# Chunk inputs of a state-space stage as four 32-row tiles on the plain input, instead of block-expanded copies of it

## The chip, the cores and the metric

The kernel runs on one core of a Trainium2 chip. The metric is the device time of one execution in microseconds (us). Engines are named as in the profile: PE is TensorE (PEld its weight loads), DVE is VectorE, ACT is ScalarE, POOL is GpSimd, SP is SyncE.

## The reference

One inference step of a two-layer decoder trunk. Layer 0 has a diagonal state-space mixer (S5), layer 1 latent attention, and each has a gated feed-forward before and behind its mixer. There are 512 prompt tokens and 8 sample tokens, 520 in all, of width 1024. Everything is float32. The change is in the mixer of layer 0:

```python
# 64 groups of 16 channels; each group has 64 complex states
ug = uf.reshape(b_, n, N_GROUPS, GROUP_CH)
x_re = jnp.einsum('bngc,gpc->bngp', ug, bb_re)
x_im = jnp.einsum('bngc,gpc->bngp', ug, bb_im)
...
_, _, s_re, s_im = lax.associative_scan(combine, (l_re, l_im, x_re, x_im), axis=1)
y = einsum(s_re, c_re) - einsum(s_im, c_im)
```

The state is carried over positions by `s = lam * s + x`. The kernel cuts the 512 positions into 64 chunks of L = 8, and first works out what each chunk adds to the state at its end: the sum over i of `lam^(7-i) * B * u[8c+i]`. These sums are the chunk inputs.

## The kernel before, in words

`u` holds the normalised input as 8 tiles t of 128 channels (8 groups, that is QP = 4 pairs of groups, of 32 channels each). Its 512 prompt columns are ordered (i, c), position in the chunk first, so that `u[:, t, i*64:(i+1)*64]` is position i of all 64 chunks; columns 512 to 519 are the sample tokens.

For each tile t four engines work in a chain:

- PE `powers_in(t)`: two matmuls of 64 rows by 512 columns (L1784), one of 64 by 128 (L1785) and two of 128 by 64 (L1787) bring the powers of lam, a factor and B into PSUM banks 4 to 6. It waits until tile t-1's were read.
- ACT copies them out (`lpz` L775, `fz` L776), DVE multiplies them (L1255 to L1267) into `bp`, and ACT spreads `bp` into the stationary operand `wb` (L782, two instructions). `wb` has two buffers by t % 2, `bp` one. DVE starts tile t when ACT has spread tile t-1.
- PE forms the chunk inputs (L1814, L1816). A stationary tile of `wb` has 128 rows (channels) and 128 columns (2 groups x 64 states). It is the same 128 columns for each of the four pairs, so a pair must see only its own 32 channels. Before, that is done by a block-expanded copy of the input, `ue`: for each of the 8 positions i, 128 rows x (4 pairs x 64 chunks), in which pair q's 64 columns are zero but for its own 32 rows. One matmul then serves four pairs. `use` is the same for the sample tokens.
- ACT copies the chunk inputs out of PSUM (`chunk_inputs`, L767 and L768). Its program has them one tile late: copies of tile t, `wb` of t, chunk inputs of t-1, copies of t+1.

DVE makes `ue` and `use` with eight copies a tile (`blocks(t)`, L1236 and L1237): those of tiles 0 and 1 ahead of the loop, those of t+1 behind the products of t. POOL clears both once (L2291), at 283 us, while PE works on the first feed-forward.

PE's order in the stage is `powers_in(0)`, and then for each t `powers_in(t+1)`, chunk inputs of t. Once four tiles are copied out, POOL scans pairs 0 to 15 (`chunk_scan`, L445 to L449); once all are, DVE scans pairs 16 to 31. PE goes on when DVE's scan is done.

A float32 matmul of the program stands in the trace as two records of PE and two of PEld. So the 8 matmuls of L1814 are 16 records.

Of the kernel before, what the change touches and what calls it, by code (L numbers as in the profile page):

```python
# [19 lines left out]
F32 = mybir.dt.float32  # L20
# [4 lines left out]
ACT = mybir.ActivationFunctionType  # L25
AX = mybir.AxisListType

P = 128
D = 1024
KD = D // P  # L30
SEQ = 512
NB = 8
TOK = SEQ + NB
# [3 lines left out]
NF = FF // P  # L37
# [6 lines left out]
L = 8  # L44
NCH = SEQ // L
NBK = 8
SCAN_T = 4
QP = 4
# [51 lines left out]
NSS = len(S_STEPS)  # L100
AFTER_CH = 2 * NPG * (R + DR) - (NQT + 2 * RT) * TOK
XQ = 48

INV2PI = 1.0 / (2.0 * math.pi)
MAGIC = 12582912.0
# [92 lines left out]
def yoco_step(nc, inp, out):  # L198
# [4 lines left out]
    with ctx:  # L203
        def take(scope, *tensors):
            return [scope.enter_context(nc.sbuf_tensor(*t)) for t in tensors]

        def sem(name):
            return ctx.enter_context(nc.semaphore(name))


        with ExitStack() as end:
            yo, yso = take(end, ("yo", [P, 4, D], F32), ("yso", [NB, D], F32))
        with ExitStack() as s:

            ue, use = take(s, ("ue", [P, 2, L, QP, NCH], F32), ("use", [P, 2, QP, NB], F32))
        xh, xl = take(ctx, ("xh", [P, KD, TOK], F32R), ("xl", [P, KD, TOK], F32R))
        x, sq, ta, tb, cst, gain, cT, kpT, ones, epsc, sd, rstd, rstc, rbc = take(
            ctx, ("x", [P, KD, TOK], F32), ("sq", [P, 2, TOK], F32), ("ta", [P, 2, TOK], F32),
# [15 lines left out]
        with ExitStack() as s:  # L234
            u, xs, bz, cz, s0, sn, lpz, fz = take(
                s, ("u", [P, KD, TOK], F32), ("xs", [P, 2, NPAIR, NCH + 1], F32), ("bz", [P, KD, 2, NS], F32),
                ("cz", [P, 2, KD, NS], F32), ("s0", [P, 2, NPAIR, NB], F32), ("sn", [P, 2, NPAIR, NB], F32),
                ("lpz", [P, 2, 2, L * NS], F32), ("fz", [P, 2, 2 * NS], F32))
            with ExitStack() as a:
                bnat, be, bp, wb, pr = take(  # L240
                    a, ("bnat", [P, 2, NPAIR, GC], F32), ("be", [P, 2, KD, P], F32), ("bp", [P, L, 2, NS], F32),
                    ("wb", [P, 2, L, 2, P], F32), ("pr", [P, 2, L * NS], F32))
# [32 lines left out]
        ps = ctx.enter_context(nc.psum_tensor("ps", [P, 8, 512], F32))  # L275


        xsm = tb[:, 0, 0:2 * NPAIR * NB].rearrange("p (r n b) -> p r n b", r=2, n=NPAIR)
# [3 lines left out]
        def prm(j, n=1):  # L282
# [19 lines left out]
        w_hi, w_lo, w_used = sem("w_hi"), sem("w_lo"), sem("w_used")  # L302
# [4 lines left out]
        std_rdy, rstd_rdy, rb_rdy = sem("std_rdy"), sem("rstd_rdy"), sem("rb_rdy")  # L307
        xn_rdy, xh_rdy, xl_rdy = sem("xn_rdy"), sem("xh_rdy"), sem("xl_rdy")
        f_sig, f_g, f_u, f_t, f_h, f_hi, f_lo, g_sig = (sem(n) for n in ("f_sig", "f_g", "f_u", "f_t", "f_h", "f_hi", "f_lo", "g_sig"))
        m_zero, d_o2, t_in, s_cz, s_ue, s_uz = sem("mla_zero"), sem("dec_o_head"), sem("trig_in"), sem("s5_ct_zero"), sem("s5_u_blocks"), sem("s5_u_zero")  # L310
        s_cpi, s_lam = sem("s5_cp_im"), sem("s5_lam_done")
        dch, ach, gch = sem("dch"), sem("ach"), sem("gch")
        pa, pd, pe_p = sem("par_act"), sem("par_dve"), sem("par_pe")
        s_in, s_tr, s_u, s_z, s_be, s_mu, s_e, s_ev, s_bb, s_bp, s_wb, s_x, s_xe = (sem("s5_" + n) for n in (
            "in", "tr", "u", "zero", "be", "mu", "lam", "lam_sb", "bb", "bp", "wb", "x", "x_sb"))
# [286 lines left out]
        def _(act):  # L602
            own = Chain(act, ach)
            run = nc.scalar.activation
# [158 lines left out]
            def chunk_inputs(t):  # L763

                act.wait_ge(s_x, t + 1)
                x_ps = ps[:, 2 * (t % 2):2 * (t % 2) + 2, :]
                run(xs[:, :, QP * t:QP * t + QP, 1:NCH + 1], x_ps[:, :, 0:QP * NCH].rearrange("p r (q c) -> p r q c", q=QP), ACT.Copy)  # L767
                run(xsm[:, :, QP * t:QP * t + QP, :], x_ps[:, :, QP * NCH:QP * (NCH + NB)].rearrange("p r (q c) -> p r q c", q=QP), ACT.Copy).then_inc(s_xe, 1)  # L768

            for t in range(KD):  # L770

# [9 lines left out]
                for h in range(2):  # L781
                    last = run(wb[:, t % 2, :, :, h * NS:h * NS + NS], bp[:, :, :, :], ACT.Copy, scale=cst[:, C_PAR + h:C_PAR + h + 1])  # L782
# [125 lines left out]
            for h in range(2):  # L908
                for r in range(RT):
                    last = run(qlat[:, r, :, h:NH:2], ps[:, 2 + h, r * NH // 2 * NB:(r + 1) * NH // 2 * NB].rearrange("p (i b) -> p b i", b=NB), ACT.Copy)  # L910
# [117 lines left out]
        def _(dve):  # L1028
            own = Chain(dve, dch)
            V = nc.vector  # L1030
            tt, stt, ts, copy = V.tensor_tensor, V.scalar_tensor_tensor, V.tensor_scalar, V.tensor_copy
# [191 lines left out]
            for w in range(2):  # L1223
                for h in range(2):
                    for c, r, sign in ((0, 0, 1.0), (1, 1, 1.0), (2, 1, -1.0), (3, 0, 1.0)):
                        first = (2 * w + r) * NG + h
                        last = ts(lst[NS * h:NS * h + NS, w, c, :], ps[0:NS, 3, first:first + NG - 1:2], sign, None, ALU.mult)
            last.then_inc(pe_p, 1)

            def blocks(t):  # L1230

                if t >= 2:
                    dve.wait_ge(s_x, t - 1)
                for q in range(QP):
                    rows = slice(32 * q, 32 * q + 32)
                    copy(ue[rows, t % 2, :, q, :], u[rows, t, 0:SEQ].rearrange("p (i c) -> p i c", i=L))  # L1236
                    last = copy(use[rows, t % 2, q, :], u[rows, t, SEQ:TOK])  # L1237
                last.then_inc(s_ue, 1)

            dve.wait_ge(s_u, KD)  # L1240
            dve.wait_ge(s_uz, 1)
            blocks(0)
            blocks(1)
            for t in range(KD):

                dve.wait_ge(s_z, t + 1)
                if t >= 1:
                    dve.wait_ge(s_wb, t)
                b_ps = ps[:, 6, P:2 * P].rearrange("p (r s) -> p r s", r=2)

                def f_(r):
                    return fz[:, t % 2, r * NS:r * NS + NS].unsqueeze(1).to_broadcast([P, 2, NS])

                q0, q1 = (pr[:, r, 0:2 * NS].rearrange("p (r s) -> p r s", r=2) for r in range(2))
                tt(q0, f_(0), b_ps, ALU.mult)  # L1255
                last = tt(q1, f_(1), b_ps, ALU.mult)
                last.then_inc(s_bb, 1)
                dve.wait_ge(s_bb, t + 1)
                tt(bz[:, t, 0, :], q0[:, 0, :], q1[:, 1, :], ALU.subtract)
                own(tt(bz[:, t, 1, :], q0[:, 1, :], q1[:, 0, :], ALU.add))  # L1260
                copy(bp[:, 0, :, :], bz[:, t, :, :])
                p0, p1 = (pr[:, r, 0:(L - 1) * NS].rearrange("p (j s) -> p j s", s=NS) for r in range(2))
                for r in range(2):
                    lam = [lpz[:, t % 2, i, 0:(L - 1) * NS].rearrange("p (j s) -> p j s", s=NS) for i in range(2)]
                    tt(p0, lam[0], bz[:, t, r:r + 1, :].to_broadcast([P, L - 1, NS]), ALU.mult)
                    own(tt(p1, lam[1], bz[:, t, 1 - r:2 - r, :].to_broadcast([P, L - 1, NS]), ALU.mult))
                    last = tt(bp[:, 1:L, r, :], p0, p1, ALU.add if r else ALU.subtract)  # L1267
                    if r == 0:
                        own(last)
                last.then_inc(s_bp, 1)  # L1270
                if 1 <= t < KD - 1:
                    blocks(t + 1)


            dve.wait_ge(s_mu, 1)
            dve.wait_ge(s_xe, KD)
# [143 lines left out]
            for k in range(4):  # L1420
                for h in range(4):
                    last = copy(qpe[DR * k:DR * k + DR, :, k, Q_POS[h]:NH:4], qq[DR * h:DR * h + DR, NH // 2:NQT, SEQ:TOK].rearrange("p g b -> p b g"))
# [133 lines left out]
            for r in range(RT):  # L1556
                own(tt(new, nwt[:, :, 0:NH], cT[:, r, SEQ:TOK].unsqueeze(2).to_broadcast([P, NB, NH]), ALU.mult))
                last = tt(olat[:, r, :, :], new, ps[:, 5 + r, 0:NB * HP].rearrange("p (b h) -> p b h", b=NB)[:, :, 0:NH], ALU.add)
# [4 lines left out]
            for h in range(2):  # L1563
                last = copy(of[DV * h:DV * h + DV, :, :],
                            ps[DV * h:DV * h + DV, 0, 0:NH * NB].rearrange("p (n b h) -> p n b h", n=NH // 2, b=NB)[:, :, :, h])
# [22 lines left out]
        def _(pe):  # L1588
            mm = nc.tensor.matmul
# [49 lines left out]
            for k in range(KD):  # L1639
                got = turn(ps[:, 5, k * NB:k * NB + NB], xsin[:, k * P:k * P + P], NB)  # L1640
# [157 lines left out]
            for t in range(KD):  # L1798
                if t + 1 < KD:
                    powers_in(t + 1)  # L1800
                pe.wait_ge(s_wb, t + 1)
                pe.wait_ge(s_ue, t + 1)
                if t == 1:
                    pe.wait_ge(pe_p, 2)
                if t >= 2:
                    pe.wait_ge(s_xe, t - 1)
                elif t == 0:
                    pe.wait_ge(s_ev, 1)


                for r in range(2):
                    x_ps = ps[:, 2 * (t % 2) + r, :]
                    for i in range(L):
                        mm(x_ps[:, 0:QP * NCH], wb[:, t % 2, L - 1 - i, r, :], ue[:, t % 2, i, :, :].rearrange("p q c -> p (q c)"),  # L1814
                           start=i == 0, stop=i == L - 1, skip_group_check=True)
                    got = mm(x_ps[:, QP * NCH:QP * (NCH + NB)], wb[:, t % 2, 0, r, :], use[:, t % 2, :, :].rearrange("p q c -> p (q c)"),  # L1816
                             start=True, stop=True, skip_group_check=True)
                got.then_inc(s_x, 1)


# [419 lines left out]
        def _(pool):  # L2240
            own = Chain(pool, gch)
            G = nc.gpsimd
# [44 lines left out]
            G.memset(prm(12), 0.0).then_inc(s_lam, 1)  # L2287


            pool.wait_ge(w_used, 2 * NF)  # L2290
            G.memset(ue[:, :, :, :, :], 0.0)  # L2291
            G.memset(use[:, :, :, :], 0.0).then_inc(s_uz, 1)
            pool.wait_ge(s_uz, 1)


            pool.wait_ge(x_upd, UPD["ffn00"] + KD)
            own(G.memset(be[:, :, :, :], 0.0))
            pool.wait_ge(s_in, 128)
# [96 lines left out]
```

## Time and profile before

| | |
|---|---|
| time, median of 3 runs (lowest, highest) | 2413.15 us (2410.35, 2415.62) |
| the profiled execution: its time, its span | 2413.23 us, 2411.6 us |
| PE, DVE, ACT, POOL busy | 2239.7, 1098.4, 774.4, 220.1 us |
| chain that ended last | PE 85%, DVE 8%, ACT 3% |
| L1814 PE, 256 records | 63.2 us |
| the stage of the change | from 430 to 531 us of the span |

The busy rows say how long each engine had something in flight. The chain is the row of instructions that ended last, followed back from the end. The granted clock (PEclk) is the share of TensorE's full 2.4 GHz: 1.00, or 0.50, which is 1.2 GHz.

### The profile page before, as it was taken

The page shows a single profiled execution, that of the slowest core. Times are in us where ns is not written, and L with a number is a line of the kernel's source. Part 1 is how long each engine was busy: PE and PEld are TensorE (multiplying, and loading weights), DVE is VectorE, ACT ScalarE, POOL GpSimd, SP SyncE. Part 2 cuts the span into 40 slices and gives each one's busy share as a digit, 9 for nine tenths or more (in the row PEclk, how much of TensorE's full clock was granted, in tenths as well). Part 3 has the DMA queues.
Part 4 walks back from the last instruction along what each step waited for, and adds up shares of the span by engine and source line. Part 5 has one row for each costly group of instructions (what it writes and reads, how often), then busy time and mean ns, then how long its engine had stood idle before and what let it go on. Part 6 is the DMA issues. An engine that isn't in the chain of part 4 may idle for free.

```text
span 2411.6 us, 45473 instructions
## 1 busy us (share of the span) xinstructions
PE 2239.7 (93%) x18959; PEld 2079.7 (86%) x18959; DVE 1098.4 (46%) x1583; ACT 774.4 (32%) x1079; POOL 220.1 (9%) x319
## 2 busy tenths in 40 slices
PE   7999999872999999999999999998898789999998
PEld 7999998651669999999999999997565579999998
DVE  5445422776553454442255444223575324445432
ACT  4343311220332444332242222224354314443311
POOL 4000000183320000000000000000004500000000
PEclk9999999795999999999999999999899979999999
DMA  4332333000003233333223333221125702332332
GB/s 118 88 95 87 104 89 76 16 0 5 2 10 97 79 88 95 90 100 94 74 87 89 96 87 107 84 72 66 46 55 141 203 27 78 88 96 87 104 86 84
DMA packets 355907, 192.30 MB, mean 80 GB/s; under 512 B 33004, under 2 KB 350442, under 8 KB 355794
## 3 DMA queue, kind: packets, MB, share of 16 engines
q1 hardware_dynamic: 348736, 180.19, 26.2%
q0 software_dynamic: 5488, 9.03, 1.4%
q10 hardware_dynamic: 1570, 1.48, 0.2%
q8 instruction: 82, 1.34, 0.2%
q14 instruction: 31, 0.25, 0.0%
HBM read 184.23 MB, written 3.02 MB: 78 GB/s over the span
## 4 chain that ended last, share of the span: by engine, by line
PE 85%; DVE 8%; ACT 3%; issue 2%; SPq 1%; DMA 1%; POOL 0%; ACTq 0%; DVEq 0%
PE ps L1602 70%; PE ps L1615 3%; PE ps L1814 2%; PE ps L1880 1%; PE ps L1944 1%; PE ps L2069 1%; DVE pr L445 1%; PE ps L2100 1%; PE ps L1831 1%; SPq L419 1%; PE ps L1621 1%; SPq L417 1%; PE ps L2047 1%; DVE wl L1039 1%; DMA cb<-cache_ckv 1%
## 5 line engine op out<-in xcount | busy, mean ns | idle before, releaser
L1602 PE MATMUL ps<-xh,wh 128*128 128x260 f32 x3296 | 869.0, 285 | 16.6 <-DVE wl L1054 8.9
L1602 PE MATMUL ps<-xl,wh 128*128 128x260 f32 x3296 | 862.3, 283 | 0.0
L1602 PE MATMUL ps<-xh,wl 128*128 128x260 f32 x3296 | 666.1, 284 | 0.0
L1602 PEld LDWEIGHTS ps<-xh,wh 128*128 128x128 f32 x3296 | 625.7, 190 | 23.7 <-issue 14.8
L1602 PEld LDWEIGHTS ps<-xl,wh 128*128 128x128 f32 x3296 | 623.8, 189 | 0.0
L1602 PEld LDWEIGHTS ps<-xh,wl 128*128 128x128 f32 x3296 | 510.9, 190 | 0.0
L640 ACT ACTIVATE wh<-raw 128x1024 fp32r<-128x1024 f32 (+1 forms) x176 | 194.3, 1104 | 609.0 <-PE ps L1602 609.0
L1602 PE MATMUL ps<-hh,wh 128*128 128x260 f32 x1408 | 370.3, 284 | 0.0
L1602 PE MATMUL ps<-hl,wh 128*128 128x260 f32 x1408 | 367.5, 282 | 0.0
L1602 PE MATMUL ps<-hh,wl 128*128 128x260 f32 x1408 | 283.3, 282 | 0.0
L1602 PEld LDWEIGHTS ps<-hh,wh 128*128 128x128 f32 x1408 | 264.9, 188 | 4.4 <-issue 4.2
L1602 PEld LDWEIGHTS ps<-hl,wh 128*128 128x128 f32 x1408 | 265.6, 189 | 0.0
L1054 DVE TENSOR_TENSOR wl<-raw,wh 128x1024 fp32r<-128x1024 f32 (+1 forms) x176 | 225.1, 1279 | 77.5 <-ACT wh L640 77.5
L1039 DVE TENSOR_TENSOR wl<-raw,wh 128x1024 fp32r<-128x1024 f32 (+1 forms) x98 | 136.0, 1387 | 231.7 <-ACT wh L622 231.7
L622 ACT ACTIVATE wh<-raw 128x1024 fp32r<-128x1024 f32 (+1 forms) x98 | 116.6, 1189 | 380.4 <-PE ps L1602 379.3
L1602 PEld LDWEIGHTS ps<-hh,wl 128*128 128x128 f32 x1408 | 217.1, 188 | 0.0
L1132 DVE TENSOR_TENSOR sq<-ps,rbc 128x520 f32<-128x520 f32 x88 | 61.6, 700 | 286.5 <-PE ps L1602 286.5
L1127 DVE TENSOR_TENSOR ta<-ps,rbc 128x520 f32<-128x520 f32 x88 | 61.6, 700 | 174.6 <-PE ps L1602 173.9
L1166 DVE SCALAR_TENSOR_TENSOR x<-ps,x 128x520 f32<-128x520 f32 (+1 forms) x32 | 22.4, 700 | 175.4 <-PE ps L1602 175.4
L700 ACT ACTIVATE hh<-ta 128x520 f32 (+1 forms) x88 | 56.4, 640 | 96.4 <-DVE ta L1136 96.4
L1814 PE MATMUL ps<-ue,wb 128*128 128x256 f32 x256 | 63.2, 404 | 7.7 <-ACT wb L782 7.7
L1814 PEld LDWEIGHTS ps<-ue,wb 128*128 128x128 f32 x256 | 50.4, 202 | 15.3 <-ACT wb L782 8.3
(362 smaller groups left out, 2219.0 us busy)
## 6 DMA issues: line engine op xcount, KB each, us to landing
raw<-ffn_w_gate SPq DMA_DIRECT2D x88, 512.0 KB, 3.9
raw<-ffn_w_up SPq DMA_DIRECT2D x88, 512.0 KB, 3.9
raw<-ffn_w_down SPq DMA_DIRECT2D x64, 704.0 KB, 4.6
cb<-cache_ckv SPq DMA_DIRECT2D x72, 128.0 KB, 2.9
cb<-cache_ckv POOLq DMA_DIRECT2D x56, 128.0 KB, 3.1
raw<-s_w_glu_v SPq DMA_DIRECT2D x8, 512.0 KB, 3.8
raw<-s_w_glu_g SPq DMA_DIRECT2D x8, 512.0 KB, 3.8
raw<-mla_w_o SPq DMA_DIRECT2D x8, 512.0 KB, 4.3
```

The costliest lines, as they stand in the source:

```text
L417: eng.dma_start(cb[j][:, g, :], inp["cache_ckv"][bass.ds(numbers[b][g], 1)].rearrange("a p r -> p (a r)")).then_inc(arrived[j], 16)
L419: eng.dma_start(kb[j][:, g, :], inp["cache_kpe"][bass.ds(numbers[b][g], 1)].rearrange("a p r -> p (a r)")).then_inc(arrived[j], 16)
L622: run(wh[par_][:, 0:size], raw[par_][:, 0:size], ACT.Copy).then_inc(w_hi, 1)
L640: run(wh[par_][:, 0:size], raw[par_][:, 0:size], ACT.Copy).then_inc(w_hi, 1)
L700: run(hh[:, bass.ds(f, 1), :].rearrange("p a t -> p (a t)"), ta[:, j, :], ACT.Copy).then_inc(f_hi, 1)
L1039: tt(wl[par_][:, 0:size], raw[par_][:, 0:size], wh[par_][:, 0:size], ALU.subtract).then_inc(w_lo, 1)
L1054: tt(wl[par_][:, 0:size], raw[par_][:, 0:size], wh[par_][:, 0:size], ALU.subtract).then_inc(w_lo, 1)
L1127: tt(halves(ta[:, j, :]), banks(0), halves(rbc[:, :]), ALU.mult).then_inc(f_g, 1)
L1132: tt(halves(sq[:, j, :]), banks(2), halves(rbc[:, :]), ALU.mult).then_inc(f_u, 1)
L1602: got = mm(ps[0:width, bank + half, 0:HALF], w[par_][:, k * width:k * width + width], src[:, k0 + k, half * HALF:half * HALF + HALF], star ...
L1615: return nc.tensor.transpose(dst, src, ident[0:rows, 0:rows])
L1814: mm(x_ps[:, 0:QP * NCH], wb[:, t % 2, L - 1 - i, r, :], ue[:, t % 2, i, :, :].rearrange("p q c -> p (q c)"), start=i == 0, stop=i == L - ...
```

## The change

`ue` and `use` are gone, with POOL's clearing and DVE's copies. PE takes the stationary and the moving operand of one pair from the same 32 rows of `wb` and of the plain `u`. So each matmul of L1814 becomes four, of 32 rows by 64 columns, and each of L1816 four of 32 rows by 8. They stand one after the other in the program, on four different row groups of the array, and write four different PSUM banks (pair q goes to bank q). All of a tile lies in columns 0 to 143 of banks 0 to 3, real part and imaginary part behind one another. Before, tiles alternated between banks 0, 1 and 2, 3. So a tile's chunk inputs now wait until ACT has copied out those of the tile just ahead, not of the one ahead of that.

```diff
+XW = NCH + NB
-            ue, use = take(s, ("ue", [P, 2, L, QP, NCH], F32), ("use", [P, 2, QP, NB], F32))
@@ ACT
-                x_ps = ps[:, 2 * (t % 2):2 * (t % 2) + 2, :]
-                run(xs[:, :, QP * t:QP * t + QP, 1:NCH + 1], x_ps[:, :, 0:QP * NCH].rearrange("p r (q c) -> p r q c", q=QP), ACT.Copy)
-                run(xsm[:, :, QP * t:QP * t + QP, :], x_ps[:, :, QP * NCH:QP * (NCH + NB)].rearrange("p r (q c) -> p r q c", q=QP), ACT.Copy).then_inc(s_xe, 1)
+                x_ps = ps[:, 0:QP, 0:2 * XW].rearrange("p q (r w) -> p r q w", r=2)
+                run(xs[:, :, QP * t:QP * t + QP, 1:NCH + 1], x_ps[:, :, :, 0:NCH], ACT.Copy)
+                run(xsm[:, :, QP * t:QP * t + QP, :], x_ps[:, :, :, NCH:XW], ACT.Copy).then_inc(s_xe, 1)
@@ DVE
-            def blocks(t):
-                if t >= 2:
-                    dve.wait_ge(s_x, t - 1)
-                for q in range(QP):
-                    rows = slice(32 * q, 32 * q + 32)
-                    copy(ue[rows, t % 2, :, q, :], u[rows, t, 0:SEQ].rearrange("p (i c) -> p i c", i=L))
-                    last = copy(use[rows, t % 2, q, :], u[rows, t, SEQ:TOK])
-                last.then_inc(s_ue, 1)
-            dve.wait_ge(s_u, KD)
-            dve.wait_ge(s_uz, 1)
-            blocks(0)
-            blocks(1)
...
-                if 1 <= t < KD - 1:
-                    blocks(t + 1)
@@ PE
-                pe.wait_ge(s_ue, t + 1)
...
-                if t >= 2:
-                    pe.wait_ge(s_xe, t - 1)
-                elif t == 0:
+                if t >= 1:
+                    pe.wait_ge(s_xe, t)
+                else:
                     pe.wait_ge(s_ev, 1)
                 for r in range(2):
-                    x_ps = ps[:, 2 * (t % 2) + r, :]
+                    c = r * XW
                     for i in range(L):
-                        mm(x_ps[:, 0:QP * NCH], wb[:, t % 2, L - 1 - i, r, :], ue[:, t % 2, i, :, :].rearrange("p q c -> p (q c)"),
-                           start=i == 0, stop=i == L - 1, skip_group_check=True)
-                    got = mm(x_ps[:, QP * NCH:QP * (NCH + NB)], wb[:, t % 2, 0, r, :], use[:, t % 2, :, :].rearrange("p q c -> p (q c)"),
-                             start=True, stop=True, skip_group_check=True)
+                        for q in range(QP):
+                            rows = slice(32 * q, 32 * q + 32)
+                            mm(ps[:, q, c:c + NCH], wb[rows, t % 2, L - 1 - i, r, :], u[rows, t, i * NCH:(i + 1) * NCH],
+                               start=i == 0, stop=i == L - 1, skip_group_check=True)
+                    for q in range(QP):
+                        rows = slice(32 * q, 32 * q + 32)
+                        got = mm(ps[:, q, c + NCH:c + XW], wb[rows, t % 2, 0, r, :], u[rows, t, SEQ:TOK],
+                                 start=True, stop=True, skip_group_check=True)
                 got.then_inc(s_x, 1)
@@ POOL
-            pool.wait_ge(w_used, 2 * NF)
-            G.memset(ue[:, :, :, :, :], 0.0)
-            G.memset(use[:, :, :, :], 0.0).then_inc(s_uz, 1)
-            pool.wait_ge(s_uz, 1)
```

On PE, at `powers_in(1)` and the chunk inputs of tile 0, there stands before (the shape is that of the output, `x8` is eight in a row):

```order
L1784 MATMUL ps<-lpw,cst 128x512 x2
L1785 MATMUL ps<-fcm,cst 128x128
L1787 MATMUL ps<-cst,be 128x64 x2
L1814 MATMUL ps<-ue,wb 128x256 x8
L1816 MATMUL ps<-use,wb 128x32
L1814 MATMUL ps<-ue,wb 128x256 x8
L1816 MATMUL ps<-use,wb 128x32
```

and in the changed kernel, whose lines are numbered 19 lower here:

```order
L1765 MATMUL ps<-lpw,cst 128x512 x2
L1766 MATMUL ps<-fcm,cst 128x128
L1768 MATMUL ps<-cst,be 128x64 x2
L1796 MATMUL ps<-u,wb 128x64 x32
L1800 MATMUL ps<-u,wb 128x8 x4
L1796 MATMUL ps<-u,wb 128x64 x32
L1800 MATMUL ps<-u,wb 128x8 x4
```

Nothing has changed places: 18 matmuls a tile have become 72. On DVE, between the products of tile 1 and those of tile 2, there stands before:

```order
L1267 TENSOR_TENSOR bp<-pr 128x7x64
L1236 COPY ue<-u 32x8x64
L1237 COPY use<-u 32x8
L1236 COPY ue<-u 32x8x64
L1237 COPY use<-u 32x8
L1236 COPY ue<-u 32x8x64
L1237 COPY use<-u 32x8
L1236 COPY ue<-u 32x8x64
L1237 COPY use<-u 32x8
L1255 TENSOR_TENSOR pr<-fz,ps 128x128
```

and in the changed kernel, where the same products are L1249 to L1251 and L1239 to L1240:

```order
L1249 TENSOR_TENSOR pr<-lpz,bz 128x448
L1250 TENSOR_TENSOR pr<-lpz,bz 128x448
L1251 TENSOR_TENSOR bp<-pr 128x7x64
L1239 TENSOR_TENSOR pr<-fz,ps 128x128
L1240 TENSOR_TENSOR pr<-fz,ps 128x128
```

Here the eight copies are gone, and tile 2's products follow tile 1's.

## Rows read from the trace of the kernel before

**Rows 1.** Stretches: PE, PEld, DVE, ACT, POOL busy (records), PEclk, DMA share, GB/s.
```profile
430.00:445.40 15.40, 10.44 (x20) 5.52 (x20) 12.83 (x42) 3.34 (x5) 8.20 (x16) 0.50 0.01 1
445.40:450.60 5.20, 5.11 (x12) 4.14 (x13) 3.92 (x10) 1.11 (x3) 0.00 (x0) 0.50 0.00 2
458.00:468.00 10.00, 10.00 (x48) 8.04 (x48) 6.55 (x19) 3.97 (x6) 0.00 (x0) 1.00 0.00 0
```

**Rows 2.** PE's timeline: start, us from first start to last end, line, records, idle before.
```profile
437.87 3.75 PE L1784 MATMUL ps<-lpw,cst 64*128 64x512 f32 x4 [2.61 <-DVE pr L1256]
...
441.98 1.11 PE L1787 MATMUL ps<-cst,be 128*128 128x64 f32 x4
445.49 6.24 PE L1814 MATMUL ps<-ue,wb 128*128 128x256 f32 x16 [2.40 <-ACT wb L782]
...
458.10 3.67 PE L1814 MATMUL ps<-ue,wb 128*128 128x256 f32 x16
...
465.52 1.98 PE L1784 MATMUL ps<-lpw,cst 64*128 64x512 f32 x4
...
468.14 3.67 PE L1814 MATMUL ps<-ue,wb 128*128 128x256 f32 x16
...
500.57 5.41 PE L1814 MATMUL ps<-ue,wb 128*128 128x256 f32 x16 [2.12 <-ACT wb L782]
```

**Rows 3.** Timeline of ACT and DVE, tile 0 and tile 2.
```profile
436.21 0.27 ACT L776 ACTIVATE fz<-ps 128x128 f32<-128x128 f32 x1
...
437.24 0.29 DVE L1255 TENSOR_TENSOR pr<-fz,ps 128x128 f32<-128x128 f32 x1
...
458.30 1.02 ACT L775 ACTIVATE lpz<-ps 128x1024 f32<-128x1024 f32 x1 [2.01 <-PE ps L1787]
...
459.52 0.29 DVE L1255 TENSOR_TENSOR pr<-fz,ps 128x128 f32<-128x128 f32 x1 [1.91 <-ACT fz L776]
...
464.28 2.19 ACT L782 ACTIVATE wb<-bp,cst 128x1024 f32<-128x1024 f32 x2 [4.79 <-DVE bp L1267]
...
466.37 0.57 ACT L767 ACTIVATE xs<-ps 128x512 f32<-128x512 f32 x1
```

**Rows 4.** Timeline of POOL, DVE and ACT, tiles 5 and 7.
```profile
487.31 1.70 POOL L445 TENSOR_TENSOR bnat<-ta,xs 128x256 f32<-128x256 f32 x2 [46.46 <-ACT tb L768]
...
489.66 0.29 DVE L1255 TENSOR_TENSOR pr<-fz,ps 128x128 f32<-128x128 f32 x1 [1.35 <-ACT fz L776]
...
498.33 2.19 ACT L782 ACTIVATE wb<-bp,cst 128x1024 f32<-128x1024 f32 x2 [8.70 <-DVE bp L1267]
...
515.90 0.29 DVE L1255 TENSOR_TENSOR pr<-fz,ps 128x128 f32<-128x128 f32 x1
...
521.03 2.19 ACT L782 ACTIVATE wb<-bp,cst 128x1024 f32<-128x1024 f32 x2 [5.61 <-DVE bp L1267]
```

**Rows 5.** Timeline: the scan of POOL and DVE, and PE behind it.
```profile
531.66 1.90 DVE L445 TENSOR_TENSOR pr<-ta,xs 128x256 f32<-128x256 f32 x2 [10.66 <-ACT tb L768]
...
556.25 1.52 POOL L2338 TENSOR_TENSOR sn<-sn,tb 128x512 f32<-128x512 f32 x1
...
564.69 1.02 DVE L445 TENSOR_TENSOR pr<-ta,xs 128x224 f32<-128x224 f32 x2
...
579.22 1.11 PE L1615 MATMUL ps<-cst,sn 128*128 128x128 f32 x4 [48.41 <-DVE xs L449]
```

**Rows 6.** L2005, pairs of 64-row tiles, elsewhere in the program.
```profile
L2005 PE MATMUL ps<-qq,ukT x64: 252/253/273, 1702.6 to 1706.1; 64*128 64x8 f32 x64
```

**Rows 7.** PE's timeline at L1873, four 32-column tiles.
```profile
606.43 2.00 PE L1873 MATMUL ps<-xs,ct 128*32 128x64 f32 x128
```

**Rows 8.** Stretches, columns as in 1: L2005; behind it; L2213 (128-row tiles, 32 columns).
```profile
1702.60:1706.30 3.70, 3.67 (x64) 3.65 (x64) 2.91 (x16) 0.00 (x0) 0.00 (x0) 1.00 0.47 109
1706.80:1712.00 5.20, 4.95 (x11) 2.29 (x12) 0.34 (x1) 1.92 (x6) 0.00 (x0) 0.50 0.56 157
...
1945.70:1952.40 6.70, 6.66 (x32) 6.66 (x32) 0.00 (x0) 0.00 (x0) 0.00 (x0) 0.50 0.00 1
```

More of the change, by code:

```diff
@@ L212, in yoco_step @@
             yo, yso = take(end, ("yo", [P, 4, D], F32), ("yso", [NB, D], F32))
-        with ExitStack() as s:
-            ue, use = take(s, ("ue", [P, 2, L, QP, NCH], F32), ("use", [P, 2, QP, NB], F32))
         xh, xl = take(ctx, ("xh", [P, KD, TOK], F32R), ("xl", [P, KD, TOK], F32R))
@@ L309, in yoco_step @@
         f_sig, f_g, f_u, f_t, f_h, f_hi, f_lo, g_sig = (sem(n) for n in ("f_sig", "f_g", "f_u", "f_t", "f_h", "f_hi", "f_lo", "g_sig"))
-        m_zero, d_o2, t_in, s_cz, s_ue, s_uz = sem("mla_zero"), sem("dec_o_head"), sem("trig_in"), sem("s5_ct_zero"), sem("s5_u_blocks"), sem("s5_u_zero")
+        m_zero, d_o2, t_in, s_cz = sem("mla_zero"), sem("dec_o_head"), sem("trig_in"), sem("s5_ct_zero")
         s_cpi, s_lam = sem("s5_cp_im"), sem("s5_lam_done")
```

## Prediction

> **What bounds the kernel now.** I read the stretches of the stage first. From 458 to 468 us, one tile, PE is busy all of 10.00 us at granted clock 1.00, while DVE has 6.55 and ACT 3.97 us of work [rows 1]. So up to tile 4 the stage goes at PE's pace. PE's timeline gives the pace: a tile's chunk inputs start at 458.10 and those of the next at 468.14, 10.04 us later [rows 2]. Of this, `powers_in` takes 2.62 (465.52 to 468.14) and the chunk inputs 7.42. The reader should also see the clock. It is 0.50 from 430 on and stays so until 450.6 [rows 1]. It has risen by the stretch at 458, and what PE ran before the rise was the first tile's chunk inputs, full 128-row matmuls of 256 columns.
>
> The second limit is the loop of ACT and DVE. For tile 2 [rows 3]: ACT's copy to DVE's first product 458.30 to 459.52, 1.22 us; products to `wb` at 464.28, 4.76; `wb` to the chunk-input copy at 466.37, 2.09; that copy about 0.8 (0.57 is its first part, the sample part behind it some 0.2). Together 8.9 us, 1.2 below PE's 10.04. From 487.31 POOL scans, and DVE's products slow down: 489.66 to 498.33, 8.67 us, for tile 5. For tile 7, when POOL is at its short instructions, they take 5.13 (515.90 to 521.03) [rows 4]. PE then waits. The stage ends into DVE's scan, which starts at 531.66 and releases PE at 579.22 [rows 5].
>
> **The change, part by part.** The profiled execution took 2413.23 us, the median of the runs is 2413.15, so the sum is made against 2413.2.
>
> 1. POOL's clearing at 283 us is gone. PE is in the first feed-forward there and waits for nothing of POOL's. Nothing.
>
> 2. DVE's copies. Those of tiles 0 and 1 lie ahead of the first product. Without them it waits for ACT's `fz`, done at 436.21 + 0.27 = 436.48, instead of starting at 437.24 [rows 3]: 0.7 us gained. The others lie beside PE's work up to tile 4. Their cover is PE's 10.04 us; should PE become short, the products could follow at once.
>
> 3. The chunk inputs on PE. A tile has 72 matmuls, so 144 records, in 36 sets of four on four row groups. The trace has no four 32-row tiles. Its nearest is L2005, 64-row tiles in alternating halves: 64 records in 3.67 us [rows 6, 8], 57 ns each. L2213, one 128-row tile after another, takes 6.66 us for 32 at clock 0.50 [rows 8], 208 ns each, so some 104 at full clock. Hence the two halves of L2005 work side by side, and each pair costs one load of 128 columns: 32 pairs at 115 ns. L1873, four 32-column tiles, has 128 records in 2.00 us, 16 ns each [rows 7], so four tiles side by side exist too. I take four at a time, a set at the price of one load, since a 32-row load has as many columns. That is 36 x 0.115 = 4.1 us at clock 1.00, and 36 x 0.208 = 7.5 at 0.50. Bounds: if the matmuls' 64 columns alone set the pace as in L1873, 144 x 16 ns = 2.3 us (4.6 at 0.50). If only two go side by side, 8.3 (15.0). If one at a time, 144 x 208 ns = 30 at 0.50.
>
> The Trainium skill (TensorE: Matmul & The Clock Gate, Back-to-back issue gap) has a rule against the change: with hardware decode off, the sequencer spends about 62 ns on each matmul. By it the tile would cost 144 x 62 ns = 8.9 us at any clock, not 4.1. The 16 ns of L1873 speak against that rule here.
>
> 4. The clock. This decides the sign. The new sets are paced by loads. Their matmuls stream 64 columns, 16 x 4 = 64 ns of every 115 by L1873's pace, so the array idles near half the time, though PE reads as busy. The trace has such streams. L2005 ran at 1.00, busy 3.67 of 3.70 us, nearly all of it loads, and the clock is 0.50 right behind it. L2213 ran 6.66 us without a gap and stayed at 0.50 [rows 8]. `powers_in`, whose long matmuls use 64 rows of the array, ran 3.75 us without a gap and stayed at 0.50 too [rows 1, 2]. The only thing that raised the clock in this stage was the 128-row stream from 445.49, and that is what is taken away. So I take 0.50 for the whole stage.
>
> 5. The sum at 0.50. `powers_in` takes 5.2 us (437.87 to 441.98 + 1.11) [rows 2], about 5.1 until the next can start. Chunk inputs 7.6 with their end. A tile: 12.7 us, against 10.04 before. Starts of the chunk inputs: tile 0 at 445.49 - 0.7 = 444.8; tile 1 at 457.5 (before 458.10, since tile 0 ran mostly at 0.50 then too); tile 4 at 457.5 + 3 x 12.7 = 495.6, before 458.10 + 3 x 10.04 = 488.2; tile 6 at 521.0, where its inputs have long been ready. Then the chain is DVE's: powers of tile 7 done about 521.1, copy 1.22, products 5.1, `wb` 2.1, chunk-input copy 0.8, so tile 7 starts at 530.4. It runs 7.9 to its result, the copy takes 0.8, and DVE's scan starts at 539.1 instead of 531.66: 7.5 us late. The new wait, for the copy of the tile just ahead, is hidden behind `powers_in`, except at tile 7, where the 0.8 stands in the sum.
>
> 6. What comes back. POOL's scan starts when tile 3 is copied, some 492.0 (`wb` of tile 4 from 489, done 491.2, then the copy) instead of 487.31: 4.7 late, while DVE's is 7.5 late. So they overlap 3 us less. Beside POOL DVE is slower: its pair of 256-column products takes 1.90 us, while 224 columns take 1.02 alone, which is 1.17 for 256, a factor of 1.63 [rows 5]. 3 us less overlap saves 3 x (1 - 1/1.63) = 1.1, and POOL, less disturbed in the slower stage, ends a little earlier still: 1.5 in all. Sum: 7.5 - 1.5 = 6 us slower, 2419.
>
> Where the clock rises behind the scan may shift: the same 16 records took 6.24 us with the rise in their course and 3.67 at full clock [rows 2], so one rise sooner or later is worth some 2.5 us either way. The forecast's own range is 2415 to 2425.
>
> **The rivals.**
>
> A. The clock rises all the same (0.15), since PE has hardly a gap. Then the loop of ACT and DVE paces the stage: 8.9 us a tile instead of 10.04, and tile 1 starts about 3.5 us earlier, as tile 0's chunk inputs shrink. By tile 4 that is 3.5 + 3 x 1.15 = 7 us, then 1 each for tiles 5 and 6, where DVE no longer copies, and 1 goes back to POOL: 8 us faster, 2405. It decides from a clock of 1.00 in about half of the stage on: each tile then gains where the forecast has it lose 2.7. Against it stand the three streams of step 4, and this: PE would now idle 8.9 - 2.6 - 4.1 = 2.2 us a tile, and after the idle 2.12 us at 500.57 sixteen records took 5.41 us instead of 3.67 [rows 2].
>
> The Trainium skill (same page, Part 1: The HAM clock gate) says that PE's activity releases the throttle and idling brings it back. If a busy PE is what it means, the stage would run at 2.4 GHz, and this rival would hold. L2213 was busy and was not released.
>
> B. Two tiles at a time, or one (0.14, of which 0.04 for one). L2005 shows two only. At 0.50 the chunk inputs take 15.0 us instead of 7.5, for eight tiles 60 more: 2413 + 6 + 60 = 2479. One at a time: 8 x 22.5 = 180 more, 2600. L1873's four column tiles speak against it.
>
> C. The loads hide and the 64 columns set the pace (0.05), 4.6 us at 0.50. A tile on PE is then 9.7, near the loop's 8.9; with the clock up the loop alone counts. Between no change and 8 us faster, 2407 as likeliest.
>
> **How the numbers follow.** The forecast has 0.66, A 0.15, B 0.14, C 0.05. What a measurement of this kernel tells from no change is about 0.2%, 4.8 us. Of the forecast's cases (6, give or take 2.5) a quarter fall within that: 0.17. So same is 0.17 and a little of C, 0.18; slower is 0.49 + 0.14 = 0.63; faster 0.19. The range leaves B out and reaches down to A: 2403 to 2425.
>
> **What the profile after would show.** PEclk 0.50 from 430 to the end of the scan (step 4). The changed L1814 in sets of four about 0.21 us apart, 7.5 us a tile (step 3). Chunk inputs 12.7 us apart, with PE busy throughout for tiles 1 to 6 (step 5). DVE's first product at 436.5 (step 2). POOL's scan starting about 492, DVE's about 539 (step 6). A clock of 1.00 there, or sets 0.4 us apart, would make the prediction wrong, each by the amount of its rival.

## The result, and the profile after

The changed kernel takes 2418.60 us (median of 17 runs, 2416.1 to 2428.3), the kernel before 2412.33 (17 runs in the same rounds, 2406.69 to 2415.82). The ratio is 1.0028, with a 95% interval of 1.0020 to 1.0036: a little slower, 6.3 us. The profiled execution of the changed kernel has a span of 2416.6 us, 5.0 more than before's 2411.6, and a mean granted clock of 0.941, where before had 0.959.

The first view is the page's row of the granted clock, one digit for each fortieth of the span (60.4 us):

```profile
PEclk9999999555999999999999999999899979999999
```

Before, the eighth, ninth and tenth digits were 7, 9 and 5. Now all three are 5. The stage ends in the ninth; the tenth belongs to the scan behind it and was 5 before too. TensorE now runs the whole stage at 1.2 GHz.

Stretches of the kernel after, columns as in [rows 1]:

```profile
430.00:445.40 15.40, 11.67 (x48) 6.71 (x48) 7.10 (x27) 4.45 (x6) 6.93 (x16) 0.50 0.01 1
445.40:450.60 5.20, 5.20 (x104) 5.20 (x101) 4.24 (x10) 0.75 (x1) 0.00 (x0) 0.50 0.02 3
458.00:468.00 10.00, 10.00 (x136) 8.28 (x133) 4.55 (x11) 3.09 (x6) 0.00 (x0) 0.50 0.01 2
450.00:535.00 85.00, 83.66 (x1037) 68.87 (x1036) 35.20 (x66) 26.52 (x40) 39.33 (x64) 0.50 0.01 2
```

PE is busy for 83.66 of 85 us and the clock stays at 0.50. In the stretch at 458 it had been 1.00 [rows 1]. In the 5.20 us from 445.40 on there are 104 matmul records, one every 50 ns.

PE's timeline of the kernel after, tiles 0 and 1, then the last two; columns as in [rows 2]:

```profile
444.04 3.69 PE L1796 MATMUL ps<-u,wb 32*128 32x64 f32 x64 [1.84 <-ACT wb L780]
...
451.83 3.78 PE L1765 MATMUL ps<-lpw,cst 64*128 64x512 f32 x4
...
457.01 3.69 PE L1796 MATMUL ps<-u,wb 32*128 32x64 f32 x64
...
521.94 3.69 PE L1796 MATMUL ps<-u,wb 32*128 32x64 f32 x64
...
531.14 3.69 PE L1796 MATMUL ps<-u,wb 32*128 32x64 f32 x64 [1.34 <-ACT tb L766]
...
584.90 1.12 PE L1596 MATMUL ps<-cst,sn 128*128 128x128 f32 x4 [45.89 <-DVE xs L447]
```

A tile's chunk inputs take 444.04 to 451.83, 7.79 us, and `powers_in` 5.18 more. The first halves of tiles 1 and 6 start 64.93 us apart, five tiles of 12.99 us, where before they were 10.04 apart [rows 2]. Only at tile 7 does PE wait. L1814 has become L1796, L1784 L1765, L1615 L1596; on DVE L1255 is L1239; on ACT and in the scans L782 and L445 are 2 lower.

The weight loads show how the sets of four go:

```profile
470.15 1.21 PEld L1796 LDWEIGHTS ps<-u,wb 32*128 32x128 f32 x20
...
L1796 PEld LDWEIGHTS ps<-u,wb x1024: 281/328/333, 444.0 to 538.2; 32*128 32x128 f32 x171
```

A load takes 328 ns, yet 20 of them take 1.21 us from the first start to the last end. Less the last one's 0.33 that is 0.88 us for four steps from set to set, 0.22 each. The four of a set start together, within some 0.02 us.

The scans, and DVE's first product:

```profile
436.35 0.29 DVE L1239 TENSOR_TENSOR pr<-fz,ps 128x128 f32<-128x128 f32 x1 [4.76 <-ACT fz L774]
...
491.98 1.46 POOL L443 TENSOR_TENSOR bnat<-ta,xs 128x256 f32<-128x256 f32 x2 [52.58 <-ACT tb L766]
...
539.88 1.98 DVE L443 TENSOR_TENSOR pr<-ta,xs 128x256 f32<-128x256 f32 x2 [11.70 <-ACT tb L766]
...
558.00 1.32 POOL L2316 TENSOR_TENSOR sn<-sn,tb 128x512 f32<-128x512 f32 x1
```

Against [rows 4, 5] POOL's scan starts 4.7 us later and ends 1.5 later. DVE's starts 8.2 later, and PE goes on 5.7 later (584.90 for 579.22). Two later lines of the kernel after show how far this delay lasts, L1989 (L2005 in the kernel before) and L2197 (L2213 there):

```profile
L1989 PE MATMUL ps<-qq,ukT x64: 252/253/273, 1708.6 to 1712.1; 64*128 64x8 f32 x64
...
L2197 PE MATMUL ps<-tb,ob x32: 401/401/422, 1950.1 to 1956.8; 128*128 128x32 f32 x32
```

At the first the kernel is 6.0 us late (before 1702.6 [rows 6]), at the second 4.4 (before 1945.7), at the end 5.0. What changes between 1700 us and the end lies in layer 1, whose program is the same in both. So 6.0 us is what the change costs in the two profiled executions, close to the 6.3 of the medians.

### The profile page after: what moved, and what is told of

It is laid out like the page before. It is cut to its first block, busy times and chain, and to the rows that moved or that the text cites. A ratio compares the mean times of both kernels' runs of the same rounds, so it can differ in the third digit from the quotient of the medians.

```text
span 2416.6 us, 47133 instructions
## 1 busy us (share of the span) xinstructions
PE 2254.0 (93%) x19823; PEld 2094.2 (87%) x19823; DVE 1072.9 (44%) x1519; ACT 774.7 (32%) x1079; POOL 211.7 (9%) x317
## 3 DMA queue, kind: packets, MB, share of 16 engines
q1 hardware_dynamic: 348736, 180.19, 26.1%
## 4 chain that ended last, share of the span: by engine, by line
PE 65%; DVE 3%; ACT 2%; SPq 1%; issue 1%; DMA 0%; DVEq 0%; ACTq 0%
PE ps L1583 54%; PE ps L1596 2%; PE ps L1928 1%; PE ps L2053 1%; PE ps L2084 1%; PE ps L1864 1%; SPq L415 1%; SPq L417 1%; PE ps L2031 1%; PE ps L1602 0%; DVE wl L1037 0%; ACT kk L921 0%; DVE mx L1423 0%; PE ps L2182 0%; PE ps L1609 0%
## 5 line engine op out<-in xcount | busy, mean ns | idle before, releaser
L1134 DVE TENSOR_TENSOR ta<-ta,sq 128x520 f32<-128x520 f32 x88 | 61.6, 700 | 3.0
L1796 PE MATMUL ps<-u,wb 32*128 32x64 f32 x1024 | 58.9, 419 | 3.2 <-ACT wb L780 1.8
```

Of the source, the lines that this page charges most:

```text
L1134: tt(ta[:, j, :], ta[:, j, :], sq[:, j, :], ALU.mult).then_inc(f_h, 1)
L1796: mm(ps[:, q, c:c + NCH], wb[rows, t % 2, L - 1 - i, r, :], u[rows, t, i * NCH:(i + 1) * NCH], start=i == 0, stop=i == L - 1, skip_group_c ...
```

## The experiments

The theory on trial: a set of four row tiles costs one load; this stream does not raise TensorE's clock, where the 128-row stream did; so the stage loses more by the clock than it gains by shorter chunk inputs. The rivals: the fineness itself costs (the number of instructions), the order of the tiles doesn't matter, or the copies on DVE mattered more than I said. x1 to x4 ran together and x5 to x8 together, each group with 23 runs of the kernel before beside it, 2413.49 and 2411.57 us in the median.

### x1_serial: the same matmuls with neighbours on the same rows

```diff
-                    for i in range(L):
-                        for q in range(QP):
-                            rows = slice(32 * q, 32 * q + 32)
-                            mm(ps[:, q, c:c + NCH], wb[rows, ...], u[rows, ...], ...)
                     for q in range(QP):
                         rows = slice(32 * q, 32 * q + 32)
+                        for i in range(L):
+                            mm(ps[:, q, c:c + NCH], wb[rows, ...], u[rows, ...], ...)
                         got = mm(ps[:, q, c + NCH:c + XW], wb[rows, ...], u[rows, t, SEQ:TOK], ...)
```

> The changed kernel with the order of its matmuls turned round: all eight positions of pair 0, then of pair 1, 2, 3, so that neighbours in the program use the same 32 rows of the array. Same matmuls, same banks. If the four-tile sets cost one load because they lie on four row groups (my reading), a tile now costs 144 x 0.208 = 30 us at clock 0.50 in place of 7.7, so eight tiles cost some 180 us more: about 2598. If what sets the pace is something else that the order doesn't touch (a fixed cost of each record, the 32-row form itself), the time stays at 2418.

Measured: 2554.63 us in one run, 136 above the changed kernel. PE's timeline, a stretch of it, and loads of one pair:

```profile
445.39 3.73 PE L1796 MATMUL ps<-u,wb 32*128 32x64 f32 x18 [1.81 <-ACT wb L780]
...
449.13 3.04 PE L1796 MATMUL ps<-u,wb 32*128 32x64 f32 x15
...
452.18 3.04 PE L1796 MATMUL ps<-u,wb 32*128 32x64 f32 x15
...
470.65 3.78 PE L1765 MATMUL ps<-lpw,cst 64*128 64x512 f32 x4
...
445.30:469.70 24.40, 24.31 (x140) 24.31 (x141) 4.55 (x11) 3.30 (x5) 0.00 (x0) 0.50 0.00 1
...
449.03 2.46 PEld L1796 LDWEIGHTS ps<-u,wb 32*128 32x128 f32 x11
```

The same 144 records take 25.3 us (445.39 to 470.65) instead of 7.79. PEld is busy throughout, and loads on the same rows follow one another: 11 in 2.46 us, less the last one's 0.33, is a step of 0.213. A whole set of four in the changed kernel takes such a step. So do 128-row loads in the kernel before, 31 steps in 6.6 us:

```profile
L2213 PEld LDWEIGHTS ps<-tb,ob x32: 288/333/333, 1945.7 to 1952.3; 128*128 128x128 f32 x32
```

Over eight tiles that is 8 x 17.5 = 140 us, and 136 were measured. So the four row groups working side by side are what makes a tile cost 7.8 us. Where my 2598 missed: a pair's 18 records take 3.05 us (449.13 to 452.18), not the 3.8 that 18 steps of 0.213 would need (3.7 with my 208 ns). At each change of rows some 0.8 us of the next pair's loads go beside the last ones of the pair ahead.

### x2_warm: the changed kernel with extra 128-row matmuls in PE's gaps

Results of the extra matmuls go to unused PSUM columns and nobody reads them. All else is computed as before.

```diff
+            def fill(n, bank=7, rows=P):
+                for _ in range(n):
+                    mm(ps[:, bank, P:3 * P], cst[0:rows, 0:P], x[0:rows, 0, 0:2 * P], start=True, stop=True, skip_group_check=True)
+            fill(7, 1)
             spread_rms("s5", SPLIT)
...
+            fill(3, 1)
             powers_in(0)
+            fill(4)
...
+                fill((10, 4, 4, 4, 4, 8, 8, 8)[t])
                 pe.wait_ge(s_wb, t + 1)
```

> The changed kernel with extra matmuls on PE whose results nobody reads: 128 rows by 256 columns, float32, in places where PE waits (7 and 3 ahead of the first powers, 4 behind them, then ahead of the chunk inputs of tiles 0 to 7: 10, 4, 4, 4, 4, 8, 8, 8). Theory: the change loses because the clock stays at 0.50 without the 128-row stream. Then these raise it to 1.00 before tile 0 and hold it; the sets come 0.11 us apart, the loop of ACT and DVE paces the stage at about 8.9 us a tile, and the time is about 2402. Rival: the row tiles are slow by themselves, or the clock can't be held over them; then the extra matmuls only lengthen PE's work and it ends at 2419 or above.

Measured: 2402.76 us (6 runs, 2399.41 to 2407.38), ratio to before 0.9963 (0.9949 to 0.9977). Stretches, then PE's timeline:

```profile
423.10:474.20 51.10, 47.30 (x703) 37.19 (x703) 32.76 (x84) 16.64 (x25) 10.93 (x21) 1.00 0.10 21
449.70:474.30 24.60, 24.53 (x480) 20.41 (x480) 13.27 (x33) 10.65 (x18) 0.00 (x0) 1.00 0.01 3
474.30:481.00 6.70, 6.70 (x16) 4.38 (x16) 1.88 (x5) 3.97 (x6) 3.12 (x5) 0.50 0.00 0
...
451.68 2.01 PE L1805 MATMUL ps<-u,wb 32*128 32x64 f32 x64
...
458.44 1.95 PE L1750 MATMUL ps<-x,cst 128*128 128x256 f32 x8
460.33 2.01 PE L1805 MATMUL ps<-u,wb 32*128 32x64 f32 x64
```

At clock 1.00 the 64 records take 2.01 us instead of 3.69, and a tile 8.65 us (451.68 to 460.33) although 1.95 of it are extras. That leaves 8.65 - 1.95 - 2.62 for `powers_in` [rows 2] = 4.1 us for a tile's chunk inputs. So at full clock the change gives a stage faster than before (10.04 a tile), and the sign hangs on the clock. The clock still fell at two places; the last of the three stretches is one. The expectation of x6_once says that PE had gaps there. At the first place it had none: in the 24.60 us ahead of the fall PE was busy for 24.53, with the row tiles, `powers_in` and four extra matmuls a tile.

### x5_fill64: the same extras on 64 rows

As x2_warm, with `rows=P // 2`.

> As the run that adds extra 128-row matmuls to the changed kernel (2402.8 us), in the same places and numbers, but each extra matmul uses 64 rows. PE is then as busy, only with half the array's rows. Theory: the powers, 64 rows too, never raised the clock, so these don't either; the clock stays at 0.50 through the stage, each extra matmul costs 0.85 us of PE's time, and with PE already the bound the whole is some 40 us longer than the changed kernel, about 2460. Rival: it is being busy without a gap that raises the clock; then as with 128 rows, about 2403.

Measured: 2458.23 us (4 runs), ratio 1.0182 (1.0158 to 1.0206). A tile's stretch, and the extras:

```profile
453.90:470.60 16.70, 16.70 (x163) 13.03 (x162) 2.25 (x8) 1.90 (x4) 0.00 (x0) 0.50 0.01 1
...
466.91 3.78 PE L1750 MATMUL ps<-x,cst 64*128 64x256 f32 x8
```

PE was busy for all of 16.70 us, and the clock was 0.50. As many matmuls with as many columns, on half of the rows, gave none of x2_warm's gain. So filled gaps by themselves don't help: with the 128-row extras the clock of this stage was at 1.00, with the 64-row extras in the same places at 0.50. A tile grew by the extras' own 3.8 us, and the whole by 40, as expected.

### x6_once: extras up to the first tile only

```diff
-                fill((10, 4, 4, 4, 4, 8, 8, 8)[t])
+                fill((10, 0, 0, 0, 0, 0, 0, 0)[t])
```

> The changed kernel with extra 128-row matmuls only up to tile 0 (7, 3, 4 and 10 of them), none after. Question: once raised, do the row tiles hold the clock? In the run with extras throughout, the clock fell to 0.50 behind tile 3 and in tile 6, where PE had gaps. Theory: without extras PE idles some 2.2 us a tile and the row tiles leave the array idle half of the rest, so the clock falls within the first tiles and nothing brings it back: 2410 to 2418. Rival: the row tiles hold it: about 2403, and the extras behind tile 0 were not needed.

Measured: 2412.73 us (10 runs), ratio 1.0006 (0.9995 to 1.0017). Stretches and PE's timeline:

```profile
436.70:453.50 16.80, 15.68 (x249) 12.58 (x252) 9.24 (x20) 7.12 (x10) 4.34 (x6) 1.00 0.00 1
453.70:462.90 9.20, 9.20 (x90) 6.79 (x86) 3.57 (x7) 2.78 (x4) 0.00 (x0) 0.50 0.00 1
475.90:532.00 56.10, 54.71 (x751) 47.17 (x750) 26.09 (x44) 15.89 (x24) 43.07 (x70) 0.50 0.01 1
...
451.68 2.01 PE L1805 MATMUL ps<-u,wb 32*128 32x64 f32 x64 [1.12 <-ACT tb L766]
...
475.91 3.69 PE L1805 MATMUL ps<-u,wb 32*128 32x64 f32 x64
```

The clock was 1.00 when the row tiles began, and fell in the course of the second. Then the pace is the changed kernel's again. The row tiles by themselves did not hold the clock here, nor did they bring it back (54.71 of 56.10 us busy at 0.50). PE had idled 1.12 us ahead of tile 1, so this run alone can't say whether they would have held it without any gap; but in x2_warm it fell once with no gap ahead. Each against the kernel before in its own rounds (1.0028, 1.0006 and 0.9963), the start alone was worth some 5 us of the 6.3 lost, and going on with the extras some 10 more.

### x3_before_warm: is the gain only that of a warm start?

The kernel before, with the same extras ahead of tile 0, and 4 each ahead of tiles 5, 6 and 7, where PE idles (`fill((10, 0, 0, 0, 0, 4, 4, 4)[t])`).

> The kernel before with the same extra matmuls up to tile 0 and 4 each ahead of tiles 5, 6, 7 (none at tiles 1 to 4, where PE has no gap). It shows what a warm start alone is worth, without the change. Expected: powers and tile 0 at clock 1.00, chunk inputs of tile 1 start about 6 us sooner, 2406. If it comes out as fast as the changed kernel with the extra matmuls (2402), the change has no gain of its own at full clock; I expect some 4 us between them.

Measured: 2413.80 us (12 runs), ratio 1.0000 (0.9988 to 1.0012). I had expected 2406. The timeline and stretches show why:

```profile
441.14 6.88 PE L1769 MATMUL ps<-x,cst 128*128 128x256 f32 x20
447.86 3.62 PE L1823 MATMUL ps<-ue,wb 128*128 128x256 f32 x16
...
439.10:445.80 6.70, 6.70 (x19) 5.06 (x18) 3.72 (x7) 2.85 (x3) 1.37 (x3) 0.50 0.00 0
446.00:530.00 84.00, 82.37 (x379) 67.13 (x378) 57.39 (x125) 26.74 (x42) 39.41 (x62) 1.00 0.00 1
```

The clock had fallen ahead of tile 0, where PE had waited for DVE, most of the extras ran at 0.50, and tile 0 started at 447.86 instead of 445.49. What it then saved at full clock (3.62 for 6.24 us [rows 2]) it had lost by starting late. From there on before had the clock at 1.00 too, but for a dip at 500.57 [rows 2], where ACT and DVE set the pace. So there was nothing left to win, whereas the row tiles had a whole stage at 0.50 to win back.

This profiled execution took 2405.01 us, 8.8 less than the median of the twelve (2404.28 to 2417.82). The stage has no part in that: PE went on behind the scan at 578.93, 0.3 us sooner than before. Two later lines show where the rest came from:

```profile
L2014 PE MATMUL ps<-qq,ukT x64: 252/253/273, 1701.7 to 1705.2; 64*128 64x8 f32 x64
...
L2222 PE MATMUL ps<-tb,ob x32: 401/401/422, 1937.6 to 1944.2; 128*128 128x32 f32 x32
```

Up to the first it was 0.9 us ahead of before (1702.6), at the second 8.1 (1945.7). Between them is attention of layer 1, the same program in both, so these 7 us are counted as scatter between executions. What extras are worth is better read at the end of the stage than from one execution's span.

### x4_nocopies: the kernel before without DVE's copies

In this kernel the chunk inputs of tiles 2 to 7 are made from the input of tiles 0 and 1; the eight copies of each later tile are left out.

```diff
-                if 1 <= t < KD - 1:
-                    blocks(t + 1)
...
-                pe.wait_ge(s_ue, t + 1)
+                pe.wait_ge(s_ue, min(t + 1, 2))
```

> The kernel before with DVE's block copies of tiles 2 to 7 left out, so the chunk inputs of those tiles are worked out from the wrong tile's data; everything else as before. It prices the part of the change that takes work off DVE. Theory: up to tile 4 the copies lie beside PE's work and cost nothing, at tiles 6 and 7 they hold DVE back by about 2 us, so 2410 to 2411, within 0.2% of before. Rival: the copies are what the stage waits for, then 4 us or more faster.

Measured: 2414.95 us (11 runs), ratio 1.0009 (1.0000 to 1.0019). Leaving DVE's copies out doesn't shorten the kernel. The timelines of DVE, PE and POOL:

```profile
502.29 0.29 DVE L1255 TENSOR_TENSOR pr<-fz,ps 128x128 f32<-128x128 f32 x1 [3.93 <-ACT fz L776]
...
513.24 6.66 PE L1812 MATMUL ps<-ue,wb 128*128 128x256 f32 x16 [2.35 <-ACT wb L782]
...
531.92 0.62 DVE L445 TENSOR_TENSOR pr<-ta,xs 128x256 f32<-128x256 f32 x1 [11.96 <-ACT tb L768]
...
554.38 1.39 POOL L2336 TENSOR_TENSOR sn<-sn,tb 128x512 f32<-128x512 f32 x1
```

DVE did begin tile 6's products at 502.29, 1.5 us sooner (503.80 before). But PE's wait for `wb` of tile 6 was 2.35 us, the clock was at 0.50 behind it, the sixteen records took 6.66 us, and DVE's scan began at 531.92, where before it was 531.66 [rows 5]. In this execution what DVE gained was lost by the clock, so the run doesn't price the copies apart from it. One thing did come of it: POOL's scan ended at 555.8 instead of 557.8 [rows 5]. It took 68.2 us (487.62 to 555.77), before 70.5 (487.31 to 557.77), and 70.4 and 70.8 in x3_before_warm and x8_before_scan, which have the copies. The copies had been slowing POOL.

### x7_warm_scan and x8_before_scan: both kernels with extras through DVE's scan too

x7 is x2_warm, x8 is x3_before_warm, both with

```diff
+            fill(104)
             pe.wait_ge(s_sn, 2)
...
             powers_out(0)
+            fill(14, 1)
             turn_out(0)
+            fill(5, 1)
```

> The changed kernel with the extras throughout the stage (2402.8 us), and more of the same kind where PE waits later: 104 during DVE's scan (44 us at full clock), 14 behind the first powers of the output part, 5 behind its first transposes. The clock should be 1.00 when the output part starts, where it is 0.50 for its first 25 us; two sets of powers, the transposes and the first taps each get 1 to 2 us shorter, together some 5: about 2397. If the extras outlast the scan or the clock falls in the gaps all the same, 2402 or above.

> The kernel before with the same extras as the run on the changed kernel with extras in the stage, the scan and the start of the output part. It shows whether the change itself, at the same clock, is worth something. The extras in the stage alone gave the kernel before nothing (2413.8 against 2413.5); those in the scan should give some 5 us: about 2408. Against 2397 for the changed kernel with them, 11 us between the two.

Measured: x7 2398.32 us (6 runs, 2393.67 to 2401.05), ratio 0.9939 (0.9923 to 0.9954), faster than both kernels; x8 2412.38 us (12 runs), ratio 0.9998 (0.9989 to 1.0007). x7, PE's timeline and a stretch:

```profile
518.68 43.11 PE L1750 MATMUL ps<-x,cst 128*128 128x256 f32 x199
...
568.14 3.78 PE L1825 MATMUL ps<-lpw,cst 64*128 64x512 f32 x4
...
584.99 1.98 PE L1825 MATMUL ps<-lpw,cst 64*128 64x512 f32 x4 [0.62 <-ACT bt L814]
586.90 3.70 PE L1852 MATMUL ps<-ct,bt 128*128 128x512 f32 x8
...
435.80:503.90 68.10, 65.24 (x1107) 53.17 (x1107) 40.00 (x77) 26.43 (x40) 29.45 (x34) 1.00 0.01 2
```

The kernel before, where those last two matmuls stand:

```profile
597.73 3.78 PE L1831 MATMUL ps<-lpw,cst 64*128 64x512 f32 x4 [2.78 <-ACT bt L816]
601.44 5.06 PE L1858 MATMUL ps<-ct,bt 128*128 128x512 f32 x8
```

In x7 the first powers behind the scan still took 3.78 us, since the clock had fallen in the 5 us of gap ahead of them; the second ones took 1.98 and the next matmuls 3.70, where before they took 3.78 and 5.06.

x8, the same two views as of x7:

```profile
447.30:580.20 132.90, 128.28 (x592) 107.21 (x590) 101.98 (x207) 27.24 (x42) 65.73 (x90) 1.00 0.00 1
...
586.13 8.49 PE L1769 MATMUL ps<-x,cst 128*128 128x256 f32 x28
```

With the clock at 1.00 in nearly all of the stage in both, the row tiles are 14 us faster than the block-expanded copies. Not all of that is the chunk inputs' own: tile 0 began at 449.56 in x8 and at 443.01 in x7. x8's own expectation, 2408, missed. As in x3, tile 0 began late, and behind the scan the clock fell all the same, so that the 28 extra records there cost 8.49 us.

## Why the prediction was right, step by step

The forecast of 2419 met 2418.6, and the mechanism was the one forecast: a set at the price of one load, at a clock that stays at 0.50. That the number met to half a microsecond is in part luck, since two terms were off and made up for each other: 7.5 - 1.5 was forecast, 8.2 - 2.5 came.

- **Steps 1 and 2, POOL's clearing and DVE's copies.** DVE's first product came at 436.35, 0.9 us sooner (0.7 predicted), and tile 0's chunk inputs at 444.04, 1.4 sooner than before (444.8 predicted). The rest is in tile 0's products, which took 5.4 us to `wb` (436.35 to 441.80) instead of 6.0 (437.24 to 443.25). That the copies beside PE's work cost nothing up to tile 4, x4_nocopies bears out: without them its tiles were 10.05 us apart there.
- **Step 3, a set of four at the price of one load.** Predicted 7.5 us a tile at clock 0.50 and 4.1 at 1.00; found 7.79 and 4.1. x1_serial shows that the row groups beside one another do it. The Trainium skill (TensorE: Matmul & The Clock Gate, Part 3: Packing small matmuls) says that a load overlaps matmuls in flight only where the row group is another. For loads on other row groups the traces agree, with 7.8 and 25.3 us for the same records. Whether a load on the same rows waits for the matmul ahead of it, no row here shows: in x1_serial it is one load after another, 0.213 us apart. Of rival B nothing is left.
- **The rule on the sequencer.** By the rule of the Trainium skill (same page, Back-to-back issue gap), 62 ns a matmul with hardware decode off, the tile was estimated at 8.9 us at any clock. The 7.79 us of the changed kernel and the 4.1 of x2_warm are below it. Which way decode was set, no run here shows.
- **Step 4, the clock.** 0.50 throughout, as said, and it decides the sign: x2_warm and x7_warm_scan are faster than before, and in x5_fill64 it stayed at 0.50 although PE was always busy. The Trainium skill (same page, Part 1: The HAM clock gate) has it that activity releases the throttle. With activity read as a busy PE, the trace disagrees: 83.66 of 85 us busy at 0.50. Rival A had its mechanism right and its condition wrong; its price, 2405, was near the 2402.8 of x2_warm, which has extras besides.
- **Step 5, the sum.** A tile takes 12.99 us, not 12.7, and DVE's scan came 8.2 us late, not 7.5. The sets are 0.216 us apart (7.79 / 36) where I had 0.208, which is 0.3 us a tile. The 0.208 was a misreading of [rows 8]: 6.66 us is the busy time of a stretch that ends before L2213's last record does. Its loads have a step of 0.213, as shown under x1_serial. From tile 1 to tile 6 that makes 5 x 0.29 = 1.5 us; tile 1 began 0.5 early (457.01 for 457.5), so tile 6 was 0.9 late against the forecast (521.94 for 521.0), and with it all that follows. The new wait for the tile just ahead cost what was said: at tile 7 `wb` was ready at 530.41 (528.22 + 2.19) and PE started at 531.14, behind ACT's copy. At full clock it counts at more tiles: in x7_warm_scan `wb` of tile 5 was ready at 488.90 and PE started at 489.64. An arrangement with two sets of PSUM columns wasn't tried.
- **Step 6, what comes back.** I had 1.5 us. It was 2.5: from DVE's start to PE's going on, 45.0 us (539.88 to 584.90), before 47.6. The term that I sized too small is the overlap with POOL. It is 19.4 us (539.9 to 559.3), before 26.1 (531.7 to 557.8): 6.7 less where I had 3, since POOL's scan itself took 67.3 us instead of 70.5. By the factor of the prediction, 6.7 x (1 - 1/1.63) = 2.6. The same factor holds elsewhere: in x7_warm_scan the overlap was 29.7 us (517.59 to 547.28) and DVE's scan up to PE's going on took 49.3 (517.59 to 566.88), so 10.3 us more overlap than in the changed kernel cost 4.3, 0.42 for each microsecond, where the factor gives 0.39. For the shorter POOL scan x4_nocopies names a cause: with the copies gone POOL's scan took 2.3 us less. The rest goes with the overlap itself: in the kernels without copies POOL's scan took 67.3, 68.3 and 70.0 us (changed kernel, x2_warm, x7_warm_scan) where DVE's overlapped it for 19.4, 24.1 and 29.7. Three profiles stand in that order, and no run changed the overlap alone.
- **The clock behind the scan** didn't shift much: PE went on 5.7 us later, and at L1989, 1100 us further on, it was 6.0 later.

## What to carry to other kernels

Row tiles on plain data remove zeros, not loads: a set of four costs one full load, and it is that cheap only if neighbours in the program stand on different row groups. Before a dense 128-row stream is thinned out, look at what the granted clock does behind it in the profile, since it may be what the clock of the whole stage hangs on; here that turned a gain of some 10 us (x2_warm) into a loss of 6. Where PE has gaps or thin streams in such a stage, extra full-row matmuls can pay for themselves, provided that they don't start at the low clock ahead of work that others wait for.

## What the runs showed of the hardware

- Matmuls of 64 rows, filling every gap, left the clock at 0.50 (x5_fill64, 16.70 of 16.70 us busy), where the same ones of 128 rows had it at 1.00 for 51.1 us (x2_warm).
- A stream of row tiles lost a clock of 1.00 within two tiles, behind one gap of 1.12 us, and did not get it back while PE was busy 54.71 of 56.10 us (x6_once). With four 128-row extras a tile it lost it once behind 24.60 us in which PE was busy for 24.53 (x2_warm).
- Four loads of 128 columns on four row groups start together, and the next four 0.22 us later at clock 0.50 (changed kernel). On the same rows one load starts every 0.213 us (x1_serial), with 32 rows in use as with 128 (L2213).
- At a change of row group some loads of the next group went beside those of the group ahead: 18 records in 3.05 us instead of 3.8 (x1_serial).
- POOL is slowed by small DVE copies of 32 rows: its scan took 68.2 us without them (x4_nocopies), 70.5 with them (before).
